# Moving routing and scatter units between the stages of a Mamba/HGRN/PEER block, and giving the gate product of the last loop to GpSimd

## Chip, cores and metric

The kernel runs on one core of a Trainium2 chip, in float32. Its engines are TensorE (PE in the rows; PEld is its weight load), VectorE (DVE), ScalarE (ACT), GpSimd (POOL) and SyncE (SP, which only issues DMAs). The metric is the device time of one execution in microseconds (us).

## The reference, cut to what matters

One block over 1024 tokens of width 1024: RMS norm, an input projection, two mixers side by side (a Mamba-2 SSD with 16 heads in 4 groups, an HGRN2 with 8 heads), an output projection with residual, then a PEER layer and a last RMS norm. The PEER layer is what the change is about:

```python
q = (xt @ w_query).reshape(t, PEER_HEADS, 2, PEER_HALF)
s = jnp.einsum('thpd,hpnd->thpn', q, sub_keys)
s_top, i_top = lax.top_k(s, 16)
cand = (s_top[:, :, 0, :, None] + s_top[:, :, 1, None, :]).reshape(t, PEER_HEADS, 256)
c_top, c_idx = lax.top_k(cand, 16)
expert = idx1 * 128 + idx2            # 16 of 16384 experts a token and head
gate = jax.nn.softmax(c_top, axis=-1)
hid = gelu(einsum('td,thkd->thk', xb, u_table[expert])) * gate
out = einsum('thk,thkd->td', hid, v_table[expert])
```

## The kernel before, in words

Tokens are 8 blocks of 128, in two halves of 4. A program of blocks, each ending when all engines have ended it, runs: norm; for each half SSD (`ssd`), HGRN (`hgrn`), output projection (`mix_out`); then the loop (`peer`). This text calls them SSD 0, HGRN 0, mix 0, SSD 1, HGRN 1, mix 1 and the loop.

**Routing.** Query and keys of one head for two token blocks are a *step* (32 steps): TensorE multiplies the queries and the scores, ScalarE copies them out. A step holds two *units* (64 units, one head of one block). VectorE picks the top 16 of a unit in three parts, `route_keys`, `route_pairs`, `route_place`, with ScalarE's `gates_act` and VectorE's `route_gates` for the softmax.

**Scatters.** The first 32 units (blocks 0 to 3, `DENSE`) are not gathered. GpSimd adds their gates into a zeroed matrix `sel` in HBM (token by expert), with 16 indirect DMAs a unit (`scatter`, L1403). This is its own stream of instructions, one after the other: 96 in mix 0, 48 at the head of SSD 1, 5 behind each of SSD 1's 16 `awide` products, 176 in HGRN 1, 112 in mix 1; 512 in all. All must be in before the loop.

**The loop.** 256 slots, in 16 groups of 16. In slots 0 to 7 of a group TensorE multiplies one tile of 128 experts' u columns with the 512 tokens of the dense half (`peer_ps_d`, L2039), ScalarE applies gelu (L2082), and the result is multiplied by the gates read back from `sel` (`peer_mt`): this is the gate product, L2176, on VectorE, from `dense`. In slots 8 to 15 it multiplies these eight tiles with the v columns into `peer_ps_o` (L2052), which VectorE adds up (L2183). Beside it, each slot handles two gathered rows of the other 32 units (`GATHER`): GpSimd fetches u and v rows of the experts into rings of 5 (`u_row` L1969, `v_row` L1977), VectorE makes a dot product (L2189) and, a slot later, a weighted sum (`combine`, L2200). Each set of 8 slots is m = 0 to 31. Before, the step of m = 0, 2, ... 18 is queried at its slot 0 and scored at its slot 4, and a unit is routed in each m = 1 to 20, its parts in slots 3, 5 and 7, the last behind the slot's combines. VectorE does the product of slot s at the start of slot s+1; TensorE waits for it at the output slot 8 (its k-th matmul there wants the k-th product).

Of the kernel before, what the change touches and what calls it, by code (L numbers as in the profile page):

```python
# [60 lines left out]
BQ = 8  # L61
GATE_LAG = 3
GRP = 4
GE = 8
# [401 lines left out]
def ssd(nc, half, S, w, w_in, w_ssd, par, w_hg, lb_logits, C, hnT, Y, spent, hw, H, state, carry, sel, sel_zeroed, R):  # L466
# [4 lines left out]
    with ExitStack() as ctx:  # L471
# [180 lines left out]
        def _(act):  # L652
# [59 lines left out]
            for n in range(first, end):  # L712
                for c in range(HC):
# [32 lines left out]
                    elif (t - first * HC) % 2 == 1 and (t - first * HC) // 2 < len(ROUTE_CHUNKS):  # L746
                        gates_act(nc, act, R, ROUTE_CHUNKS[(t - first * HC) // 2])

        @block.vector
        def _(dve):  # L750
# [89 lines left out]
            for n in range(first, end):  # L840
# [7 lines left out]
                for c in range(HC):  # L848
# [88 lines left out]
def hgrn(nc, half, G, w_hg, w_out, C, hnT, Y, osq, ysq, first_w, hw, H, state, sel, R):  # L937
# [6 lines left out]
    with ExitStack() as ctx:  # L944
# [132 lines left out]
        def _(act):  # L1077
# [34 lines left out]
            for m in range(first, end):  # L1112
                if m == deep:
                    ken_out(m * HC)
                for c in range(HC):
# [12 lines left out]
                    square_out(t)  # L1128
                    if c == HC - 1 and m < first + HC:
# [9 lines left out]
        def _(dve):  # L1139
            prep = Own(dve, H.own_prep, 1)  # L1140
            for held in atts:
                ins = nc.vector.memset(held[:], 0.0)
# [45 lines left out]
            for m in range(first, end):  # L1188
# [6 lines left out]
                for c in range(HC):  # L1195
# [47 lines left out]
class Route:  # L1243
# [151 lines left out]

def scatter(nc, pool, R, sel, n, ks):
# [36 lines left out]
def mix_out(nc, half, M, x, w_out, mix_w, ffn_w, w_route, u_cols, sel, sel_zeroed, first_w, hw, C, Y, osq, ysq, hnT, R, ut):  # L1433
# [4 lines left out]
    with ExitStack() as ctx:  # L1438
# [10 lines left out]
        if half == 0:  # L1449
# [9 lines left out]
                "p (j a k) -> p j a k", j=2, a=2) for i in range(SCORES - 1))]  # L1459
        else:  # L1460
# [32 lines left out]
        def _(sp):  # L1493
# [39 lines left out]
            load_queries(step + 3)  # L1533
            load_x(first + 3)
            load_keys(step + 3)
            loads(step + 4)
            key_loads(step + 4)
            loads(step + 5)
            key_loads(step + 5)
            for i in TAIL:  # L1540
                load_queries(i)
                load_keys(i)

        @block.tensor
        def _(pe):
# [57 lines left out]
            for b in range(first, end):  # L1603
# [745 lines left out]
```

## Time and profile before

| | us |
|---|---|
| median of 3 runs | 3754.54 (3753.33 to 3755.51) |
| profiled execution, time | 3756.04 |
| profiled execution, span | 3754.3 |
| PE busy | 3378.3 (90%) |
| DVE busy | 2653.5 (71%) |
| POOL busy | 2061.6 (55%) |
| ACT busy | 913.5 (24%) |

The time is 1.7 us above the span of the trace. Busy shares are averages over stages with different limits, so the table alone doesn't say which engine ends a stage. TensorE's granted clock over the whole span is 0.949 of full speed.

### The profile page before, as it was taken

The page shows a single profiled execution, that of the slowest core. Times are in us where ns is not written, and L with a number is a line of the kernel's source. Part 1 is how long each engine was busy: PE and PEld are TensorE (multiplying, and loading weights), DVE is VectorE, ACT ScalarE, POOL GpSimd, SP SyncE. Part 2 cuts the span into 40 slices and gives each one's busy share as a digit, 9 for nine tenths or more (in the row PEclk, how much of TensorE's full clock was granted, in tenths as well). Part 3 has the DMA queues.
Part 4 walks back from the last instruction along what each step waited for, and adds up shares of the span by engine and source line. Part 5 has one row for each costly group of instructions (what it writes and reads, how often), then busy time and mean ns, then how long its engine had stood idle before and what let it go on. Part 6 is the DMA issues. An engine that isn't in the chain of part 4 may idle for free.

```text
span 3754.3 us, 36373 instructions
## 1 busy us (share of the span) xinstructions
PE 3378.3 (90%) x10816; PEld 1900.1 (51%) x10816; DVE 2653.5 (71%) x6220; ACT 913.5 (24%) x2301; POOL 2061.6 (55%) x1618
## 2 busy tenths in 40 slices
PE   7999997992999998197599999999999999999998
PEld 4666774581566777154244444444444444444443
DVE  2476663598698666027488787878787888777888
ACT  3334452220234444022112111111111111111112
POOL 1000000187867788788665555556555656666765
PEclk9999998996999998598799999999999999999999
DMA  3453112253422343342799999999999999999998
GB/s 119 157 219 140 51 57 110 61 117 47 68 46 34 57 63 40 54 97 33 251 378 388 350 348 353 387 355 352 352 385 347 339 375 401 388 402 396 401 404 333
DMA packets 370772, 868.60 MB, mean 231 GB/s; under 512 B 97552, under 2 KB 192016, under 8 KB 363408
## 3 DMA queue, kind: packets, MB, share of 16 engines
q0 software_dynamic: 221184, 537.23, 42.7%
q1 hardware_dynamic: 127840, 246.60, 18.2%
q10 hardware_dynamic: 21552, 82.45, 5.6%
q8 instruction: 87, 1.43, 0.2%
q14 instruction: 109, 0.89, 0.1%
HBM read 828.14 MB, written 38.01 MB: 231 GB/s over the span
## 4 chain that ended last, share of the span: by engine, by line
PE 39%; DMA 5%; DVE 4%; issue 2%; POOL 1%; ACT 0%; DVEq 0%; ACTq 0%; POOLq 0%
PE peer_ps_o L2052 22%; PE peer_ps_d L2039 15%; DMA peer_vr<-in_v_rows,index_g 5%; PE peer_ps_q L2002 2%; DVE Y L2200 1%; DVE peer_ur L2189 1%; POOL peer_ur L1969 0%; DVE lists L1362 0%; DVE route_chosen L1364 0%; DVE lists L1360 0%; POOL peer_vr L1977 0%; DVE Y L2176 0%; DMA wk<-in_w_route 0%; DVE route_ix L1326 0%; DVE route_ix L1318 0%
## 5 line engine op out<-in xcount | busy, mean ns | idle before, releaser
L1403 POOL DMA_INDIRECT sel<-lists x512 | 836.8, 1634 | 292.9 <-issue 151.9
L1969 POOL DMA_INDIRECT peer_ur<-in_u_rows,index_g x512 | 564.1, 1102 | 523.6 <-DVE peer_ur L2189 396.4
L2200 DVE SCALAR_TENSOR_TENSOR Y<-peer_vr,osq,Y 128x1024 f32<-128x1024 f32 x512 | 657.8, 1285 | 143.0 <-DMA peer_vr<-in_v_rows,index_g 142.8
L1977 POOL DMA_INDIRECT peer_vr<-in_v_rows,index_g x512 | 599.2, 1170 | 235.1 <-issue 146.0
L2189 DVE SCALAR_TENSOR_TENSOR peer_ur<-peer_ur,Y 128x1024 f32<-128x1024 f32 x512 | 629.2, 1229 | 43.4 <-DMA peer_ur<-in_u_rows,index_g 43.2
L2052 PE MATMUL peer_ps_o<-hw,Y 128*128 128x512 f32 x1024 | 466.2, 615 | 55.1 <-DVE Y L2176 55.1
L2052 PE MATMUL peer_ps_o<-hnT,Y 128*128 128x512 f32 x1024 | 442.7, 592 | 0.0
L2052 PEld LDWEIGHTS peer_ps_o<-hw,Y 128*128 128x128 f32 x1024 | 201.1, 198 | 315.6 <-issue 249.5
L2052 PEld LDWEIGHTS peer_ps_o<-hnT,Y 128*128 128x128 f32 x1024 | 194.4, 190 | 243.9 <-issue 243.5
L2039 PE MATMUL peer_ps_d<-hnT,held 128*128 128x512 f32 x688 | 302.3, 592 | 0.0
L2039 PE MATMUL peer_ps_d<-hnT,state 128*128 128x512 f32 x688 | 302.3, 592 | 0.0
L2039 PE MATMUL peer_ps_d<-hnT,peer_ut 128*128 128x512 f32 x672 | 295.2, 592 | 0.0
L580 PE MATMUL ssd_ps_piece<-hnT,w_group 128*128 128x512 f32 x512 | 233.2, 610 | 67.9 <-DMA w_group<-in_w_ssd 56.3
L2082 ACT ACTIVATE Y<-peer_ps_d 128x512 f32<-128x512 f32 x128 | 76.4, 597 | 802.4 <-PE peer_ps_d L2039 802.4
L2089 ACT ACTIVATE osq<-osq 128x2 f32<-128x2 f32 x256 | 51.1, 200 | 757.7 <-DVE peer_ur L2189 757.5
L2039 PEld LDWEIGHTS peer_ps_d<-hnT,state 128*128 128x128 f32 x688 | 130.5, 190 | 161.4 <-issue 161.2
L2039 PEld LDWEIGHTS peer_ps_d<-hnT,held 128*128 128x128 f32 x688 | 130.4, 190 | 161.4 <-issue 161.2
L2039 PEld LDWEIGHTS peer_ps_d<-hnT,peer_ut 128*128 128x128 f32 x672 | 127.5, 190 | 158.0 <-issue 157.8
L2176 DVE TENSOR_TENSOR Y<-Y,peer_mt 128x512 f32<-128x512 f32 x128 | 88.5, 691 | 153.4 <-ACT Y L2082 152.5
L580 PEld LDWEIGHTS ssd_ps_piece<-hnT,w_group 128*128 128x128 f32 x512 | 99.9, 196 | 189.6 <-issue 132.2
L559 POOL TENSOR_TENSOR ssd_awide<-ssd_a,tri 128x512 f32<-128x512 f32 x32 | 38.4, 1202 | 284.9 <-PE ssd_ps_rows L630 238.9
L1024 PE MATMUL hg_ps_piece<-hnT,hw 128*128 128x512 f32 x384 | 172.4, 602 | 0.3 <-DMA hw<-in_w_hg 0.3
(335 smaller groups left out, 4775.7 us busy)
## 6 DMA issues: line engine op xcount, KB each, us to landing
sel<-Y ACTq DMA_DIRECT2D x16, 2048.0 KB, 7.1
peer_mt<-sel ACTq DMA_DIRECT2D x64, 512.0 KB, 8.5
hw<-in_v_cols SPq DMA_DIRECT2D x16, 2048.0 KB, 10.9
hnT<-in_v_cols SPq DMA_DIRECT2D x16, 2048.0 KB, 13.9
state<-in_u_cols SPq DMA_DIRECT2D x43, 512.0 KB, 7.7
held<-in_u_cols SPq DMA_DIRECT2D x43, 512.0 KB, 7.7
peer_ut<-in_u_cols SPq DMA_DIRECT2D x42, 512.0 KB, 8.0
w_group<-in_w_ssd SPq DMA_DIRECT2D x32, 512.0 KB, 4.1
```

Of the source, the lines that this page charges most:

```text
L580: mm = nc.tensor.matmul(bank, w[:, k, i * P:(i + 1) * P], hnT[:, half, k, :], start=(k == 0), stop=(k == KT - 1))
L1024: mm = nc.tensor.matmul(bank, w[:, kt, p * P:(p + 1) * P], hnT[:, half, kt, :], start=(kt == 0), stop=(kt == KT - 1))
L1403: nc.gpsimd.indirect_dma_start(sel.rearrange("a i q two (t o) -> (a i q two t) o", o=1), bass.IndirectOffsetOnAxis(ap=R.index_d[:, at, k:k ...
L1969: nc.gpsimd.indirect_dma_start(ur[:, r % RING, :], None, u_rows, bass.IndirectOffsetOnAxis(ap=R.index_g[:, r // TOPK % RQ, r % TOPK:r % TO ...
L1977: nc.gpsimd.indirect_dma_start(vr[:, r % RING, :], None, v_rows, bass.IndirectOffsetOnAxis(ap=R.index_g[:, r // TOPK % RQ, r % TOPK:r % TO ...
L2002: mm = nc.tensor.matmul(ps_q[:, p, :], wq[:, k, p * P:(p + 1) * P], xg[:, k, :], start=(k == 0), stop=(k == KT - 1))
L2039: mm = nc.tensor.matmul(ps_d[:, e % 2, 0:DT], ut[e % UT][:, k, :], xT[:, k, 0:DT], start=(k == 0), stop=(k == KT - 1))
L2052: mm = nc.tensor.matmul(ps_o[:, o % OB, :], ht(e, tb), v_tile(e, side), start=(j == 0), stop=(j == GE - 1))
L2082: nc.scalar.activation(ht(e), ps_d[:, e % 2, 0:DT], ACT.Gelu).then_inc(gelu_done, 1)
L2176: nc.vector.tensor_tensor(h, h, m_tile(e), ALU.mult).then_inc(h_made, 1)
L2189: nc.vector.scalar_tensor_tensor(out=ur[:, s, :], in0=ur[:, s, :], scalar=1.0, in1=Y[:, b, D:MIX], op0=ALU.mult, op1=ALU.mult, accum_out=d ...
L2200: nc.vector.scalar_tensor_tensor(out=hb, in0=vr[:, s, :], scalar=hid[:, c:c + 1], in1=hb, op0=ALU.mult, op1=ALU.add).then_inc(comb_done, 1)
```

## The change

Constants move routing and scatters between the stages, and the code around them follows:

| units of | mix 0 | head of SSD 1 | chunks of SSD 1 | HGRN 1 | mix 1 | loop |
|---|---|---|---|---|---|---|
| routing before | 22 | 4 + 2 | 4 | 0 | 12 | 20 |
| routing after | 14 | 5 + 2 | 5 and a third | 5 and two thirds | 6 | 26 |
| scatters before | 6 | 3 | 5 | 11 | 7 | 0 |
| scatters after | 5 | 3 | 7 | 10 | 7 | 0 |

The steps multiplied in mix 1 fall from 6 to 3, those of the loop rise from 10 to 13. In mix 0 all 16 steps stay; scores of its last 8 now go to places of their own (`later`), so ScalarE needn't wait until VectorE has picked from them. In SSD 1 and HGRN 1 a chunk takes one third of a unit (`part_dve`) where it took half a unit in the first 8 chunks of SSD 1. In the loop the gate product goes from VectorE's `dense` to GpSimd's `gate_product`; a step is queried in odd m, so at slot 8 of a group, and scored at slot 12, and the loads of query weights move with it.

```diff
-BQ = 8
+BQ = 12
-ROUTED_STEPS = HALF_STEPS + 6
-ROUTED_IN = [range(0, 22), range(UNITS // 2, 2 * ROUTED_STEPS)]
-ROUTE_BEFORE, ROUTE_AFTER, ROUTE_CHUNKS = range(22, 26), range(26, 28), range(28, 32)
-SCATTER_MIX0, SCATTER_PROLOGUE, SCATTER_SSD = DENSE[0:6], DENSE[6:9], DENSE[9:14]
-SCATTER_CHUNK = 5
-SCATTER_HG, SCATTER_MIX1 = DENSE[14:25], DENSE[25:]
+ROUTED_STEPS = HALF_STEPS + 3
+ROUTED_IN = [range(0, 14), range(UNITS // 2, 2 * ROUTED_STEPS)]
+ROUTE_BEFORE, ROUTE_AFTER, ROUTE_CHUNKS = range(14, 19), range(19, 21), range(21, UNITS // 2)
+SCATTER_MIX0, SCATTER_PROLOGUE, SCATTER_SSD = DENSE[0:5], DENSE[5:8], DENSE[8:15]
+SCATTER_CHUNK = 7
+SCATTER_HG, SCATTER_MIX1 = DENSE[15:25], DENSE[25:]
...
+def part_dve(nc, dve, R, q):
+    if q // 3 < len(ROUTE_CHUNKS):
+        n = ROUTE_CHUNKS[q // 3]
+        if q % 3 == 0:
+            route_keys(nc, dve, R, n)
+        elif q % 3 == 1:
+            route_pairs(nc, dve, R, n)
+        else:
+            route_place(nc, dve, R, n)
+            route_gates(nc, dve, R, n)
...
-        TURN_AT = 3
+        TURN_AT = 2 * (3 * PH - ROUTED_STEPS)
...
             i = first_step + m // 2
-            return i if m % 2 == 0 and i < STEPS else None
+            return i if m % 2 == 1 and i < STEPS else None
...
-            n = 2 * first_step - 1 + m
-            return n if m >= 1 and n < UNITS else None
+            n = 2 * first_step - 2 + m
+            return n if m >= 2 and n < UNITS else None
...
+            def gate_product(e):
+                pool.wait_ge(gelu_done, e + 1)
+                if e % 2 == 0:
+                    pool.wait_ge(m_in[e // 2 % 2], 16 * (e // 4 + 1))
+                h = ht(e).rearrange("p (q t) -> p q t", t=SELB)
+                nc.gpsimd.tensor_tensor(h, h, m_tile(e), ALU.mult).then_inc(h_made, 1)
...
-            for p in range(PAIRS):
+            for p in range(PAIRS + 1):
+                if p > 0 and (p - 1) % SLOTS < GE:
+                    gate_product((p - 1) // SLOTS * GE + (p - 1) % SLOTS)
                 for r in (2 * p + RING, 2 * p + 1 + RING):
...
             def dense(q):
                 g, s = q // SLOTS, q % SLOTS
-                if s < GE:
-                    e = g * GE + s
-                    dve.wait_ge(gelu_done, e + 1)
-                    if e % 2 == 0:
-                        dve.wait_ge(m_in[e // 2 % 2], 16 * (e // 4 + 1))
-                    h = ht(e).rearrange("p (q t) -> p q t", t=SELB)
-                    nc.vector.tensor_tensor(h, h, m_tile(e), ALU.mult).then_inc(h_made, 1)
-                else:
+                if s >= GE:
```

TensorE at the start of the loop, before (a row is a run of like instructions; `held`, `state` and `peer_ut` are the three places of u columns, `hw` and `hnT` hold the v columns, `peer_ps_q` is the query, `peer_ps_s` the score):

```order
L2002 MATMUL peer_ps_q<-xg,wk 128x256 x16
L2039 MATMUL peer_ps_d<-hnT,state 128x512 x8
L2039 MATMUL peer_ps_d<-hnT,held 128x512 x8
L2039 MATMUL peer_ps_d<-hnT,peer_ut 128x512 x8
L2039 MATMUL peer_ps_d<-hnT,state 128x512 x8
L2012 MATMUL peer_ps_s<-wk,reset 128x128 x4
L2039 MATMUL peer_ps_d<-hnT,held 128x512 x8
L2039 MATMUL peer_ps_d<-hnT,peer_ut 128x512 x8
L2039 MATMUL peer_ps_d<-hnT,state 128x512 x8
L2039 MATMUL peer_ps_d<-hnT,held 128x512 x8
L2052 MATMUL peer_ps_o<-hw,Y 128x512 x32
L2052 MATMUL peer_ps_o<-hnT,Y 128x512 x32
```

The same engine at the same place, after the change (the last eight rows of the group):

```order
L2049 MATMUL peer_ps_d<-hnT,held 128x512 x8
L2049 MATMUL peer_ps_d<-hnT,peer_ut 128x512 x8
L2049 MATMUL peer_ps_d<-hnT,state 128x512 x8
L2049 MATMUL peer_ps_d<-hnT,held 128x512 x8
L2012 MATMUL peer_ps_q<-xg,wk 128x256 x16
L2062 MATMUL peer_ps_o<-hw,Y 128x512 x32
L2022 MATMUL peer_ps_s<-wk,reset 128x128 x4
L2062 MATMUL peer_ps_o<-hnT,Y 128x512 x32
```

The query has moved from ahead of the first u tile to between the last u tile and the first output, and the score to the middle of the outputs.

GpSimd in the loop, before, in any slot:

```order
L1969 DMA peer_ur<-in_u_rows,index_g 128x1024 x2
L1977 DMA peer_vr<-in_v_rows,index_g 128x1024 x2
L1969 DMA peer_ur<-in_u_rows,index_g 128x1024 x2
L1977 DMA peer_vr<-in_v_rows,index_g 128x1024 x2
L1969 DMA peer_ur<-in_u_rows,index_g 128x1024 x2
```

GpSimd in the loop after the change, the last two of a group's eight products and the first slot without one:

```order
L1988 TENSOR_TENSOR Y<-Y,peer_mt 128x512
L1970 DMA peer_ur<-in_u_rows,index_g 128x1024 x2
L1978 DMA peer_vr<-in_v_rows,index_g 128x1024 x2
L1988 TENSOR_TENSOR Y<-Y,peer_mt 128x512
L1970 DMA peer_ur<-in_u_rows,index_g 128x1024 x2
L1978 DMA peer_vr<-in_v_rows,index_g 128x1024 x2
L1970 DMA peer_ur<-in_u_rows,index_g 128x1024 x2
```

The product of a slot stands ahead of the four gathers issued in the next one, and behind those of its own.

## Rows read from the trace of the kernel before

**Rows 1.** Busy time by stretch, HGRN 1 (columns named in the first line).
```profile
core 0: us, PE busy (x) PEld busy (x) DVE busy (x) ACT busy (x) POOL busy (x), PEclk, DMA share, GB/s
1240.00:1510.00 270.00, 253.41 (x1294) 195.57 (x1292) 176.21 (x560) 125.06 (x264) 228.53 (x137) 0.95 0.36 51
1510.00:1585.00 75.00, 2.13 (x10) 1.57 (x9) 1.28 (x4) 0.37 (x2) 57.25 (x38) 0.51 0.23 6
```

**Rows 2.** GpSimd in order of time: start us, us, engine, line, what [idle before].
```profile
733.71 1.82 POOL L1403 DMA_INDIRECT sel<-lists  x1 [122.06 <-DVE lists L1393]
...
918.66 1.55 POOL L1403 DMA_INDIRECT sel<-lists  x1 [0.30 <-issue]
927.13 1.55 POOL L1403 DMA_INDIRECT sel<-lists  x1 [6.92 <-POOLq L1438]
...
1211.63 1.03 POOL L559 TENSOR_TENSOR ssd_awide<-ssd_a,tri 128x512 f32<-128x512 f32 x1 [2.81 <-PE ssd_ps_rows L630]
...
1234.80 1.55 POOL L1403 DMA_INDIRECT sel<-lists  x1 [11.13 <-POOLq L471]
...
1576.99 1.55 POOL L1403 DMA_INDIRECT sel<-lists  x1 [0.30 <-issue]
...
1596.44 1.57 POOL L1403 DMA_INDIRECT sel<-lists  x1 [0.16 <-issue]
...
1810.20 1.55 POOL L1403 DMA_INDIRECT sel<-lists  x1 [0.30 <-issue]
```

**Rows 3.** VectorE in order of time: first instruction of one unit and of the next.
```profile
739.06 0.48 DVE L1315 MAX8 route_ti<-Y 128x8 f32<-128x128 f32 x2
...
748.77 0.48 DVE L1315 MAX8 route_ti<-Y 128x8 f32<-128x128 f32 x2
```

**Rows 4.** VectorE in order of time, head of SSD 1.
```profile
974.73 0.53 DVE L783 COPY hw<-carry 128x12 f32<-128x12 f32 x1 [10.14 <-ACT ssd_rawz L666]
```

**Rows 5.** Busy time by stretch, loop: columns as in rows 1.
```profile
1818.00:1833.40 15.40, 9.62 (x33) 8.11 (x34) 2.47 (x4) 1.28 (x1) 10.81 (x11) 0.65 0.95 382
1833.40:3192.84 1359.44, 1304.37 (x3201) 607.05 (x3201) 1104.63 (x1945) 237.78 (x740) 789.42 (x700) 0.98 0.96 366
3192.84:3742.50 549.66, 549.60 (x1281) 242.76 (x1279) 439.40 (x576) 91.14 (x303) 363.09 (x314) 1.00 1.00 392
```

**Rows 6.** Busy time by stretch: a group with a query, a group without.
```profile
2825.30:2953.84 128.54, 120.57 (x298) 56.51 (x297) 102.39 (x185) 22.12 (x68) 72.36 (x65) 0.96 0.94 353
3247.78:3357.64 109.86, 109.86 (x257) 48.63 (x257) 86.67 (x113) 14.94 (x56) 73.00 (x65) 1.00 1.02 404
```

**Rows 7.** Chain that ended last: start us, us, what.
```profile
2953.84 6.91 PE peer_ps_q L2002 x32
```

**Rows 8.** TensorE in order of time, in the same group.
```profile
2859.51 1.05 PE L2012 MATMUL peer_ps_s<-wk,reset 128*128 128x128 f32 x8
...
2902.01 24.36 PE L2052 MATMUL peer_ps_o<-hw,Y 128*128 128x512 f32 x50 [7.97 <-DVE Y L2176]
```

**Rows 9.** VectorE in order of time, in the same group.
```profile
2839.74 0.69 DVE L2176 TENSOR_TENSOR Y<-Y,peer_mt 128x512 f32<-128x512 f32 x1 [6.86 <-ACT Y L2082]
...
2883.68 1.28 DVE L2200 SCALAR_TENSOR_TENSOR Y<-peer_vr,osq,Y 128x1024 f32<-128x1024 f32 x1 [4.03 <-DMA peer_vr<-in_v_rows,index_g]
...
2890.84 1.22 DVE L2189 SCALAR_TENSOR_TENSOR peer_ur<-peer_ur,Y 128x1024 f32<-128x1024 f32 x1 [2.93 <-DMA peer_ur<-in_u_rows,index_g]
...
2896.39 1.28 DVE L2200 SCALAR_TENSOR_TENSOR Y<-peer_vr,osq,Y 128x1024 f32<-128x1024 f32 x1 [4.32 <-DMA peer_vr<-in_v_rows,index_g]
```

**Rows 10.** Costliest groups: busy us, mean ns | idle before, releaser.
```profile
L2176 DVE TENSOR_TENSOR Y<-Y,peer_mt 128x512 f32<-128x512 f32 x128 | 88.5, 691 | 153.4 <-ACT Y L2082 152.5
```

**Rows 11.** GpSimd, then VectorE, in order of time, in SSD 1.
```profile
1109.20 1.22 POOL L559 TENSOR_TENSOR ssd_awide<-ssd_a,tri 128x512 f32<-128x512 f32 x1 [3.31 <-PE ssd_ps_rows L630]
...
1109.44 1.90 DVE L1360 TENSOR_TENSOR Y<-route_count_u,route_place 128x864 f32<-128x864 uint32 x1
...
1139.01 1.05 DVE L1360 TENSOR_TENSOR Y<-route_count_u,route_place 128x864 f32<-128x864 uint32 x1
```

More of the change, by code:

```diff
@@ L1128, in _ @@
                     square_out(t)
+                    if half == 1:
+                        part_act(nc, act, R, GROUPS * HC + t - first * HC)
                     if c == HC - 1 and m < first + HC:
@@ L1140, in _ @@
             prep = Own(dve, H.own_prep, 1)
+            R.own.eng = dve
             for held in atts:
@@ L1203, in _ @@
                         attend(t + 1)
+                    if half == 1:
+                        part_dve(nc, dve, R, GROUPS * HC + t - first * HC)
                     advance(t)
@@ L1285, in scores @@
     def scores(self, i):
-        return self.slots[i % SCORES] if i < HALF_STEPS else self.sc[:]
+        if i >= HALF_STEPS:
+            return self.sc[:]
+        return self.slots[i % SCORES] if i < PH else self.later[i - PH]
 def hit_of(ap):
@@ L1305, in scores_free @@
 def scores_free(i):
-    return 2 * (i - SCORES + 1) if i < HALF_STEPS else 2 * i
+    if i >= HALF_STEPS:
+        return 2 * i
+    return 2 * (i - SCORES + 1) if i < PH else 0
 def route_keys(nc, dve, R, n):
@@ L1459, in mix_out @@
                 "p (j a k) -> p j a k", j=2, a=2) for i in range(SCORES - 1))]
+            R.later = [Y[:, i // 2, D + i % 2 * HALF:D + (i % 2 + 1) * HALF].rearrange("p (j a k) -> p j a k", j=2, a=2)
+                       for i in range(PH)]
         else:
@@ L1481, in mix_out @@
         step = half * HALF_STEPS
-        EARLY_STEPS = range(step, step + 6)
         TAIL = range(step + 6, HALF_STEPS) if half == 0 else range(0)
+        MORE = half == 0
         w_in = [first_w, *M.w_in]
@@ L1532, in _ @@
             load_keys(step + 2)
-            load_queries(step + 3)
+            if MORE:
+                load_queries(step + 3)
             load_x(first + 3)
[L1535 to L1542, printed above, removed]
+            if MORE:
+                load_keys(step + 3)
+                for i in range(step + 4, HALF_STEPS):
+                    load_queries(i)
+                    load_keys(i)
         @block.tensor
@@ L1651, in _ @@
                 score(i - 1)
-            score(step + 5 + len(TAIL))
+            if MORE:
+                score(HALF_STEPS - 1)
         @block.scalar
@@ L1728, in _ @@
                     x_copy(b - 1, 1)
-                if at == HC - 1:
+                if at == HC - 1 and MORE:
                     query_out(step + 3)
                     gates(unit + 4)
-                    if half == 0:
-                        x_copy(b - 1, 1)
+                    x_copy(b - 1, 1)
                 if at + 1 < HC:
@@ L1754, in _ @@
                 score_out(i - 1)
-                if i > TAIL[0]:
-                    gates(done)
-                    done += 1
-            score_out(step + 5 + len(TAIL))
-            for n in range(done, unit + len(ROUTED_IN[half])):
+            if MORE:
+                score_out(HALF_STEPS - 1)
+            for n in range(unit + 6, unit + len(ROUTED_IN[half])):
                 gates(n)
@@ L1817, in _ @@
                     scale_y(b + 2)
-                if at == HC - 1:
-                    route(unit + 6)
                 dve.wait_ge(M.h_squared, past(b + 1))
@@ L1822, in _ @@
                                         ALU.add).then_inc(M.h_meaned, 1)
-                if at == HC - 1:
-                    route(unit + 7)
                 dve.wait_ge(M.h_rooted, past(b + 1))
@@ L1833, in _ @@
             routed = unit + len(ROUTED_IN[half])
-            for n in range(unit + 8, routed):
+            for n in range(unit + 6, routed):
                 route(n)
-            for n in range(routed - GATE_LAG, routed):
+            for n in range(max(unit, min(routed - GATE_LAG, unit + 6)), routed):
                 route_gates(nc, dve, R, n)
```

46 lines of the change are left out of this document (16 added, 30 removed).

## Prediction

> **What bounds the kernel now.** I read the busy time by stretch first, then for each stretch the engine that ends it, then the chain that ended last in the loop.
>
> In HGRN 1 the arithmetic is over at 1510, and until 1585 only GpSimd works, 57 of 75 us [rows 1]: the block waits for scatters. In order of time GpSimd issues them almost without a break from 733.7 on: mix 0's 96 until 918.7, then a change of block with 6.9 us idle, 176 in HGRN 1 from 1234.8 to 1577.0, 112 in mix 1 from 1596.4 to 1810.2 [rows 2]. The reader is to see pitches of (918.66 - 733.71) / 95 = 1.95 us in mix 0, 342.2 / 175 = 1.955 in HGRN 1 and 213.8 / 111 = 1.93 in mix 1. Mix 0, HGRN 1 and mix 1 end with their scatters; SSD 1 is set by its chunks, 8 of them from 1109.20 [rows 11] to 1211.63 [rows 2], 12.8 us each.
>
> The loop runs from 1818.0 to 3742.5, 1924.5 us [rows 5]. From 3192.8 TensorE never pauses: 549.6 us of work in 549.66 us, and a group without a query takes 109.86 us [rows 5, 6]. Before that, groups with routing lose time. A query is 6.91 us [rows 7], a score about 0.9 (1.05 with its modelled end [rows 8]), so a group with both should take 117.7 us; the one shown takes 128.5, with 8.0 us of TensorE idle [rows 6]. The idle time ends on VectorE's gate product (7.97 us), and the 50 matmuls behind it take 24.4 us [rows 8], where 50 at the later pace (109.86 / 256 = 0.429) take 21.5; the group's granted clock is 0.96 against 1.00 [rows 6]. Over the stretch up to 3192.84: 11 groups of 109.86, 9 queries, 10 scores and some 2 us of transposes make 1281.7 us of 1359.4; 77.7 us are lost, 55.1 idle and 22.6 at a slower clock [rows 5].
>
> Why the product is late: in the group shown VectorE waits 4.03, 2.93 and 4.32 us for gathered rows, then routes a third of a unit, then comes to the eighth product [rows 9]. Earlier in the group it had waited 6.86 us itself, for gelu, as the query stood ahead of the first tile [rows 9]. VectorE is busy 102.4 of those 128.5 us [rows 6]. The two wait for each other in turn.
>
> **Change, part by part.**
>
> *Mix 0.* One unit fewer to scatter: 16 x 1.95 = 31.2 us off the end, if nothing else ends later. VectorE had 8 units more than now, at 748.77 - 739.06 = 9.71 us each [rows 3], so its tail falls by 78 us and stays behind GpSimd's. TensorE keeps its 16 steps; its score copies lose a wait. -31.
>
> *Head of SSD 1.* A fifth unit ahead of the group's preparation, 9.7 us. VectorE idles 10.1 us there for ScalarE's copies [rows 4]: this hides it. 0, and up to +10 if ScalarE came early.
>
> *Chunks of SSD 1.* GpSimd's chunk becomes 1.2 us of `awide` with its gap and 7 scatters at 1.91 us: 14.6 us. Its first block instruction to the sixteenth `awide` is 927.1 to 1211.6, 284.5 us [rows 2]. With 48 scatters at 1.90 (91 us) and 15 chunks of 14.6 (219) it is 310, +25.5 us. VectorE takes 3.2 us of routing a chunk in place of 4.9 in the first eight, 3.2 in place of 0 in the rest; GpSimd's 14.6 us covers it, except perhaps in the last chunk. +26.
>
> *HGRN 1.* 160 scatters for 176: -16 x 1.955 = -31.3. The routing added, 5 and two thirds units or 55 us, lies in 17 of 32 chunks. VectorE is busy 176 of 270 us and TensorE 253 [rows 1]; the arithmetic is over 67 us before the last scatter, and would still be over some 10 us before it if all of the 55 came on top. Sum up to mix 1: -31 + 26 - 31 = -36; 1 us back for the last chunk. **-35**.
>
> *Mix 1.* VectorE loses 6 units (58 us), TensorE three steps; both lie beside the 112 scatters, which stay. At best the pitch falls from 1.93 to the 1.85 of undisturbed ones (1.55 + 0.30 [rows 2]), -9; I take **-2**.
>
> *Loop, TensorE's work.* Three queries and scores more: 3 x 7.8 = +23.4. The start needs no query weights: now 15.4 us pass before the first tile, 9.6 of them a slow first query [rows 5]; the wait of 5.8 goes, the slow clock falls on the first tile (2.7 over a warm query). Work after: 16 x 109.86 + 13 x 7.8 + 2.7 + 2 + 1 = 1865 us.
>
> *Loop, what becomes of the 77.7 us.* The query now lies between the eighth tile and the first output, and in that output seven eighths can run before the eighth product is wanted: 12.9 us of cover, where it was 6. In the group shown the combines of slot 7 end at 2897.6, 9.7 us after the eighth tile. GpSimd then has one or two gathers and the product: about 2.5 us, 12.2 in all. VectorE's place-part no longer stands ahead. It just fits, without any gain in the waits for rows; moving the 1 MB of query weights away from slot 6 should make these shorter.
>
> *Loop, VectorE.* It gives up 8 products a group at 0.69 us [rows 10] (0.6 apart in sequence), -4.8. But GpSimd's product makes VectorE wait: beside `awide` (same size, 1.22 us) a VectorE product took 1.90 us, where its like takes 1.05 [rows 11], so 0.85 us a product, +6.8. A group with routing is 102.4 - 4.8 + 6.8 = 104 us of 117.7; 13 us are left for the 11.3 of waits for rows. The Trainium skill, SBUF — State Buffer, Who interferes with whom, says that a VectorE instruction with two SBUF inputs and a GpSimd one that reads SBUF exclude each other, the second fully blocked. By that rule the price is the whole 1.22 us, 9.8 a group: 107 of 117.7, and the sum stays; this trace shows 0.85. The same skill, GPSIMD Engine Reference, Engine selection, advises against two-input products on GpSimd, about twice as slow; the trace has 1.03 to 1.22 us against 0.69.
>
> *Loop, GpSimd.* Busy 72.4 us and 65 gaps of 0.3 make 92 of 128.5 [rows 6, 2]; 8 products with gaps at 1.2 to 1.4 add 11: 103 of 117.7, or of 109.9 in late groups. It has room, but little. Bound of the product from above: 1.22 plus a wait of 1.28 for VectorE's instruction, 8 x 2.5 = 20, 112 us, still below 117.7 and over 109.9.
>
> *Transfers.* The late group moves 404 GB/s with a DMA share of 1.0 over 109.86 us, 44.4 MB [rows 6]. With 1.1 MB of query in 117.7 us it is 387 GB/s, so it fits too.
>
> I leave 1.5 us a routing group (13 x 1.5 = 20) for what is left of stalls and slow clock: 1865 + 20 = 1885, **-40** (0 a group gives -60, 4.5 a group -1). Sum: -35 - 2 - 40 = -77. The profiled execution, 3756.0 with its 1.7 us outside the span, would be 3679; it lies 1.5 above the median of the runs, which goes from 3754.5 to **3677**.
>
> **Rivals.**
> 1. *The stall stays, as it is made by transfers.* For it: three near-full engines and a DMA share near 1, and 13 groups that route instead of 10. Against it: the cover doubles. With 3 to 6 us a group the loop is 1904 to 1943, -20 to +19: 3697 to 3736.
> 2. *Slower: GpSimd becomes the loop's bound.* Its queue is in order: a product waits for gelu, four gathers wait behind it, VectorE for their rows, the next product for VectorE. It decides if a routing group takes 7.5 us over 117.7 (13 x 7.5 = 97, eating 37 + 60), which is a pitch of 125.2, as now. At 128.5 the time is 3754.5 - 37 + 81 = 3799. For it: 103 to 112 us of work in order. Against it: gathers now wait for VectorE's dot at the same place anyway.
> 3. *Front part falls short.* HGRN 1's arithmetic is stretched past its scatters, or the chunks take 16 us: 10 to 20 lost, 3687 to 3697.
> 4. *More than forecast:* no stall left, scatters at 1.85 us: 3754.5 - 42 - 9 - 62 = 3642.
> 5. *It does nothing of what it says:* gains cover only the added queries. That is rival 1 at its end.
>
> **How the numbers follow.** Forecast with rival 3 (3655 to 3697) 0.65; rival 4, below 3655, 0.08; rival 1 0.17; rival 2 0.10, most of it above 3762. The range 3640 to 3720 leaves out rival 2, half of rival 1 and little else. Some 0.2%, 7.5 us, is what a measurement here can tell. Faster by more: 0.65 + 0.08 + 0.16 = 0.89; within: 0.03; slower: 0.08.
>
> **What would show it.** Mix 0's last scatter near 888; `awide` 14.6 apart in SSD 1; HGRN 1's last scatter near 1541, with 10 to 40 us of GpSimd alone before it; mix 1 as long as before, VectorE idle at its end; the loop's routing groups at 118 to 120 us with a clock of 1.00, VectorE's instructions near the products 0.6 to 0.9 longer. I am wrong if TensorE still waits at slot 8, if a product on GpSimd takes over 2.5 us, or if groups without routing exceed 110 us.

## The result: 3713.4 us, faster by 1.0%, and the profile after

| | before | after |
|---|---|---|
| median of runs, us | 3753.93 (3747.84 to 3755.51, 4 runs) | 3713.43 (3711.16 to 3720.9, 4 runs) |
| ratio, 95% interval | | 0.9899 [0.9881, 0.9916] |
| profiled execution: time, span | 3756.04, 3754.3 | 3720.9, 3719.2 |
| start of the loop (after: of its first tile), us | 1818.0 | 1786.13 |
| loop to the last matmul | 1924.5 | 1921.2 |

The change gains 40.5 us where 77 were forecast, and 3677 lies below all of its runs. The profiled execution is the slowest of the four, 7.5 us over their median; I come back to that.

**Front.** GpSimd in order of time, after: the first scatter of SSD 1, the sixteenth `awide`, the first and last scatter of HGRN 1, the last of mix 1, the first gather. They answer to [rows 2].

```profile
893.82 1.55 POOL L1420 DMA_INDIRECT sel<-lists  x1 [5.77 <-POOLq L1455]
...
1202.85 1.61 POOL L559 TENSOR_TENSOR ssd_awide<-ssd_a,tri 128x512 f32<-128x512 f32 x1
...
1228.66 1.57 POOL L1420 DMA_INDIRECT sel<-lists  x1 [10.25 <-POOLq L471]
...
1547.56 1.55 POOL L1420 DMA_INDIRECT sel<-lists  x1 [0.31 <-issue]
...
1778.18 1.55 POOL L1420 DMA_INDIRECT sel<-lists  x1 [0.30 <-issue]
1786.85 1.01 POOL L1970 DMA_INDIRECT peer_ur<-in_u_rows,index_g  x1 [7.12 <-POOLq L1455]
```

SSD 1 begins at 893.8 where it was 927.1, so mix 0 gave 33 us (forecast 31). The sixteenth `awide` is 309 us behind it (forecast 310, was 284.5), and no idle time stands before it any more: GpSimd sets the chunks. HGRN 1's last scatter is at 1547.6, where 1541 was forecast; its pitch is (1547.56 - 1228.66) / 159 = 2.006 us, not 1.955, 8 us over 159 scatters. That is a matter of this execution: in e1, the same instructions up to the loop, it is 1.96 us (1228.8 to 1540.5).

Busy time by stretch, HGRN 1 after, against [rows 1]:

```profile
core 0: us, PE busy (x) PEld busy (x) DVE busy (x) ACT busy (x) POOL busy (x), PEclk, DMA share, GB/s
1500.00:1530.00 30.00, 9.19 (x69) 8.49 (x69) 10.47 (x42) 3.68 (x13) 25.12 (x17) 0.67 0.22 1
1530.00:1550.00 20.00, 0.00 (x0) 0.00 (x0) 0.00 (x0) 0.00 (x0) 16.07 (x11) 0.50 0.23 0
```

From 1530 on GpSimd works alone: the routing put into HGRN 1 stayed beside the scatters, which still end the block.

**Loop.** Busy time by stretch after, in order: the first group, a usual one, that with the transposes, the last three. Against [rows 6]:

```profile
1786.00:1919.70 133.70, 124.16 (x297) 57.70 (x298) 83.11 (x101) 17.41 (x59) 92.85 (x79) 0.93 0.99 388
1919.70:2037.36 117.66, 117.66 (x297) 55.61 (x297) 101.73 (x171) 22.34 (x68) 84.67 (x72) 1.00 0.99 380
...
2391.07:2516.46 125.39, 120.08 (x313) 56.94 (x313) 104.51 (x177) 23.94 (x72) 89.38 (x76) 1.00 0.97 369
...
3344.91:3468.11 123.20, 114.34 (x257) 49.77 (x257) 103.17 (x177) 21.56 (x66) 88.23 (x74) 0.94 0.95 361
3468.11:3589.15 121.04, 111.67 (x257) 49.07 (x257) 92.35 (x115) 19.99 (x64) 90.14 (x73) 0.96 0.96 373
3589.15:3707.30 118.15, 112.82 (x257) 49.26 (x255) 92.23 (x113) 26.46 (x71) 83.04 (x66) 0.97 0.89 323
```

Seven of the routing groups came down to the 117.7 us that their work takes, as forecast, with TensorE never idle and the granted clock at 1.00 in the one shown; four more take 118.4 to 119.9. What is new is mostly at the ends: the first group takes 133.4 us, and groups without a query, which had taken 109.9 us [rows 6], now take 118 to 123. TensorE in order of time in the first of them, against [rows 8]:

```profile
3399.68 5.31 PE L2062 MATMUL peer_ps_o<-hw,Y 128*128 128x512 f32 x12
3408.84 2.07 PE L2062 MATMUL peer_ps_o<-hw,Y 128*128 128x512 f32 x2 [3.85 <-POOL Y L1988]
3415.92 24.72 PE L2062 MATMUL peer_ps_o<-hw,Y 128*128 128x512 f32 x50 [5.01 <-POOL Y L1988]
```

TensorE waits for the seventh product, and again for the eighth, now for GpSimd: 8.9 us. The other 4.5 us over 109.9 go with the granted clock, 0.94 in that group where it was 1.00. Costliest groups after, columns as in [rows 10]:

```profile
L2203 DVE SCALAR_TENSOR_TENSOR Y<-peer_vr,osq,Y 128x1024 f32<-128x1024 f32 x512 | 690.6, 1349 | 178.3 <-DMA peer_vr<-in_v_rows,index_g 124.5 <-issue 53.4
L2192 DVE SCALAR_TENSOR_TENSOR peer_ur<-peer_ur,Y 128x1024 f32<-128x1024 f32 x512 | 675.3, 1319 | 109.1 <-DMA peer_ur<-in_u_rows,index_g 107.8 <-DVE route_place L1355 0.2
```

In the kernel with the product back on VectorE (e1, below) the same two take 1282 and 1229 ns. The difference is 512 x (67 + 90) ns = 80 us, 0.63 us for each of the 128 products.

Here is what each group of the loop takes, from the start of its first u tile to that of the next one, in us, for all kernels of this study (an edit of each is told below):

| kernel | 0 | 1 to 12, those over 118.0 | 13 | 14 | 15 | loop |
|---|---|---|---|---|---|---|
| before | 117.8 | 123.6 to 128.5 in 1 to 8; 117.2, 114.9, then 109.9 | 109.9 | 110.1 | 110.0 | 1909.2 |
| after | 133.4 | 125.4 (5), 118.4 to 119.9 in four | 123.2 | 121.0 | 118.3 | 1921.2 |
| e1, product on VectorE | 126.5 | 125.4 (5) | 118.8 | 109.9 | 110.0 | 1884.9 |
| e2, that in 13 to 15 | 132.8 | 123.8 (4), 125.4 (5), 118.2 (11) | 117.9 | 109.9 | 110.0 | 1898.1 |
| e3, before + product on GpSimd | 120.4 | 116.7 to 129.1 | 118.7 | 116.9 | 118.2 | 1949.8 |
| e4, before + query in odd m | 127.4 | 125.4 (2); 113.0 (10), 109.9 (11, 12) | 109.9 | 110.0 | 110.0 | 1856.7 |
| e5, e1 + transposes in m = 9 | 126.4 | 119.4 (4) | 118.4 | 109.9 | 110.0 | 1878.5 |
| e6, two fills for the product | 129.4 | 125.4 (5) | 122.0 | 116.4 | 110.0 | 1897.6 |
| e7, half of the products on GpSimd | 125.8 | 125.4 (5), 119.1 (6) | 120.3 | 113.9 | 110.0 | 1891.8 |
| e8, front moves alone | 117.7 | 122.8 to 127.2 in 1 to 11, 115.9 (12) | 116.5 | 109.9 | 110.0 | 1942.0 |
| e9, e5 + parts in slots 1, 3, 5 | 126.4 | 119.4 (4) | 109.9 | 114.8 | 110.0 | 1874.9 |
| e10, after + transposes in m = 9 | 133.9 | 120.2 (5), 118.2 to 119.9 in seven | 120.6 | 122.6 | 117.2 | 1915.6 |

(Before, e3 and e8 begin with a query ahead of the first tile, 6.9 us and more, which the last column leaves out for them: 1909.2 is 1924.5 less 15.3, and those are the wait for the query weights and the query itself.)

### The profile page after: what moved, and what is told of

Its sections match the earlier page's. It is cut to its first block, busy times and chain, and to the rows that moved or that the text cites. A ratio compares the mean times of both kernels' runs of the same rounds, so it can differ in the third digit from the quotient of the medians.

```text
span 3719.2 us, 36340 instructions
## 1 busy us (share of the span) xinstructions
PE 3382.6 (91%) x10816; PEld 1901.5 (51%) x10816; DVE 2690.8 (72%) x6092; ACT 928.7 (25%) x2312; POOL 2312.7 (62%) x1746
## 4 chain that ended last, share of the span: by engine, by line
PE 41%; issue 3%; DMA 3%; POOL 3%; DVE 2%; ACT 0%; POOLq 0%; ACTq 0%; DVEq 0%
PE peer_ps_o L2062 23%; PE peer_ps_d L2049 16%; DMA peer_vr<-in_v_rows,index_g 3%; PE peer_ps_q L2012 1%; POOL peer_ur L1970 1%; DVE Y L2203 1%; POOL Y L1988 1%; POOL peer_vr L1978 1%; PE peer_ps_s L2022 0%; DVE peer_ur L2192 0%; DVE Y L2220 0%; PE peer_ps_t L2031 0%; ACT xg L2086 0%; DVE wk L2220 0%; ACT osq L2103 0%
## 5 line engine op out<-in xcount | busy, mean ns | idle before, releaser
L1970 POOL DMA_INDIRECT peer_ur<-in_u_rows,index_g x512 | 636.9, 1244 | 334.6 <-DVE peer_ur L2192 218.8
L2203 DVE SCALAR_TENSOR_TENSOR Y<-peer_vr,osq,Y 128x1024 f32<-128x1024 f32 x512 | 690.6, 1349 | 178.3 <-DMA peer_vr<-in_v_rows,index_g 124.5
L2192 DVE SCALAR_TENSOR_TENSOR peer_ur<-peer_ur,Y 128x1024 f32<-128x1024 f32 x512 | 675.3, 1319 | 109.1 <-DMA peer_ur<-in_u_rows,index_g 107.8
L2062 PE MATMUL peer_ps_o<-hw,Y 128*128 128x512 f32 x1024 | 455.5, 604 | 37.2 <-POOL Y L1988 37.2
L580 PE MATMUL ssd_ps_piece<-hnT,w_group 128*128 128x512 f32 x512 | 232.6, 608 | 48.5 <-DMA w_group<-in_w_ssd 36.4
```

Of the source, the lines that this page charges most:

```text
L580: mm = nc.tensor.matmul(bank, w[:, k, i * P:(i + 1) * P], hnT[:, half, k, :], start=(k == 0), stop=(k == KT - 1))
L1970: nc.gpsimd.indirect_dma_start(ur[:, r % RING, :], None, u_rows, bass.IndirectOffsetOnAxis(ap=R.index_g[:, r // TOPK % RQ, r % TOPK:r % TO ...
L2062: mm = nc.tensor.matmul(ps_o[:, o % OB, :], ht(e, tb), v_tile(e, side), start=(j == 0), stop=(j == GE - 1))
L2192: nc.vector.scalar_tensor_tensor(out=ur[:, s, :], in0=ur[:, s, :], scalar=1.0, in1=Y[:, b, D:MIX], op0=ALU.mult, op1=ALU.mult, accum_out=d ...
L2203: nc.vector.scalar_tensor_tensor(out=hb, in0=vr[:, s, :], scalar=hid[:, c:c + 1], in1=hb, op0=ALU.mult, op1=ALU.add).then_inc(comb_done, 1)
```

## The experiments

Theory T1, formed from the trace after: wherever no query lies between the last u tile and the first output, GpSimd's eighth product comes late, because four gathers and a product a slot take GpSimd more than TensorE's 6.87 us; and beside each product VectorE loses time. Rivals: R1, handing the product over is what gained, and the late groups are its price; R2, transfers set the pace.

**e1: the product back on VectorE, all else changed.**

```diff
-                if p > 0 and (p - 1) % SLOTS < GE:
+                if False:
                     gate_product((p - 1) // SLOTS * GE + (p - 1) % SLOTS)
...
-                if s >= GE:
+                if s < GE and True:
+                    e = g * GE + s
+                    dve.wait_ge(gelu_done, e + 1)
...
+                    nc.vector.tensor_tensor(h, h, m_tile(e), ALU.mult).then_inc(h_made, 1)
```

> The changed kernel with one part undone: the gate product is back on VectorE in all groups, at the start of the next slot; queries stay in odd m and all moves between stages stay. Theory T1 (GpSimd's queue, with four gathers and a product a slot at a pitch of about 8.0 us against TensorE's 6.87, delivers the eighth product late wherever no query lies in between, and makes VectorE's instructions longer): the last three groups return from 118 to 123 us to 109.9, -33, the first group gives some 5 back, the routing groups keep their 12.9 us of cover and lose at most 1 us each as VectorE is slower by 4.8 us of products but quicker by 5 us of blocked port: 3670 to 3690, so faster than the changed kernel's 3713. Rival R1 (the routing groups need the product off VectorE, and it was the handover that gained): they go back to some 125 us, 12 x 7 = +84, less 33: 3755 to 3765. Rival R2 (transfers set the loop): 3710 to 3715.

Measured: 3671.29 us (3666.95 to 3678.7), ratio 0.9789 [0.9768, 0.9811]. R1 and R2 fall: with the product where it was, groups 1 to 12 take 117.7 us but for that with the transposes, and the last two 109.9 and 110.0. T1's time came true, though group 13 stayed at 118.8 us where it had 109.9. Handing the product to GpSimd costs 3713 - 3671 = 42 us by the medians. The medians of the kernel before that were timed beside the two differ by 4.9 us of this (3753.9 and 3749.0), which leaves 37, and the loops of the two profiled executions differ by 36.3.

**e2: the product on VectorE in groups 13 to 15 alone.** The two conditions read `(p - 1) // SLOTS < 13` and `g >= 13`.

> The changed kernel, with the gate product on VectorE in groups 13 to 15 alone (the three without a query), on GpSimd in groups 0 to 12. T1: these three take 109.9 us each again in place of 123.2, 121.0 and 118.2, so -33: 3680, TensorE's granted clock there 1.00 and no wait at slot 8. R2 (the late groups are slow as their rows and tiles come late): 3710 to 3715, with waits for DMA in these groups.

Measured: 3685.53 us (3677.12 to 3687.75), ratio 0.9822 [0.9801, 0.9843], 5.5 us over T1's 3680. The last two groups are at 109.9 and 110.0, group 13 at 117.9. The three gave 24.7 us, not 33: 8 us of group 13's delay are not GpSimd's (TensorE waits 5.8 us there for VectorE's eighth product; see e9). In groups 1 to 12 GpSimd's products cost little: e2 is 6.1 us longer than e1 in group 4 and 1.4 us in the other eleven together; 6.3 more are in group 0.

**e3: the kernel before with the product on GpSimd alone.** The inverse of e1's edit, on the kernel before.

> The kernel before, with one part of the change: the gate product on GpSimd; queries stay in even m and nothing moves between stages. T1: the six groups without a query, which took 109.9 us, take 118 to 123, +50 to +75, and the routing groups, whose query stands ahead of the first tile and covers nothing, gain nothing: 3800 to 3830, slower. R1 (handing the product to GpSimd is what gained): routing groups 118 in place of 125, 10 x 7 = -70, late groups up by 60: 3740 to 3750. If the product on GpSimd costs nothing by itself: 3690.

Measured: 3801.18 us (3787.22 to 3804.86), ratio 1.0132 [1.0109, 1.0154]: slower, as T1 has it. Groups 11 to 15 take 117 to 119 us in place of 109.9 to 110.1, and groups 0 to 9 together gain 4 us.

**e4: the kernel before with the query in odd m alone.**

```diff
-        TURN_AT = 3
+        TURN_AT = 4
...
-            return i if m % 2 == 0 and i < STEPS else None
+            return i if m % 2 == 1 and i < STEPS else None
...
-            n = 2 * first_step - 1 + m
-            return n if m >= 1 and n < UNITS else None
+            n = 2 * first_step - 2 + m
+            return n if m >= 2 and n < UNITS else None
```

> The kernel before, with one part of the change: queries in odd m, so between the last u tile and the first output, with the units and the transposes following; the product stays on VectorE and nothing moves between stages. T1: the cover for the eighth product grows from 6 to 12.9 us, the stalls of some 8 us in ten groups mostly go, and the clock with them: -50 to -75: 3680 to 3705. R1 (only the handover helps): 3750 to 3757.

Measured: 3689.09 us (3681.72 to 3690.7), ratio 0.9837 [0.9818, 0.9856]. These few lines give 60 us, one and a half times what the whole change gives.

**e5: e1 with the transposes in m = 9.** `TURN_AT = 9`.

> As the kernel with all products on VectorE (median 3671), and the four groups of transposes moved from m = 10 (slots 2 to 5, where TensorE computes u tiles and ScalarE has a gelu in each slot) to m = 9 (slots 10 to 13, as before the change). Theory T2 (the transposes wait for ScalarE's copies, which stand behind gelu there; 125.4 us for that group against 117.7): the group returns to some 118.5 us, -7: 3664. Rival (transposes cost some 8 us anywhere in the group with a query at slot 8): 3671.

Measured: 3663.42 us (3660.73 to 3671.18), ratio 0.9787 [0.9771, 0.9803]. The group that now holds them, 4, takes 119.4 us, and group 5 is back at 117.7: 1.7 us for what took 7.7. TensorE in order of time in the changed kernel's group 5 shows what is saved: ScalarE copies each set out only behind its gelu, and TensorE waits to overwrite it.

```profile
2413.88 0.66 PE L2031 MATMUL peer_ps_t<-ident,Y 128*128 128x128 f32 x4 [1.77 <-ACT xg L2086]
2414.37 7.03 PE L2049 MATMUL peer_ps_d<-hnT,held 128*128 128x512 f32 x16
2423.17 0.66 PE L2031 MATMUL peer_ps_t<-ident,Y 128*128 128x128 f32 x4 [1.77 <-ACT xg L2086]
```

**e6: fills in place of the product.** The gate product is left out, so the outputs are of a constant.

```diff
                 h = ht(e).rearrange("p (q t) -> p q t", t=SELB)
-                nc.gpsimd.tensor_tensor(h, h, m_tile(e), ALU.mult).then_inc(h_made, 1)
+                nc.gpsimd.memset(m_tile(e), 0.5)
+                nc.gpsimd.memset(h, 0.5).then_inc(h_made, 1)
```

> The changed kernel with the gate product left out altogether: in its place in GpSimd's queue, behind the same waits and with the same release, stand two fills with a constant, of the gates' tile and of the activations' tile, which read no SBUF (a fill of this size takes 0.52 us in the trace of before, so some 1.1 us for both against the product's 1.35). The output tiles are then computed from a constant. It splits T1 in two. T1a (time in GpSimd's queue alone makes the eighth product late): late groups stay at 116 to 121 us, 3700 to 3710. T1b (what costs is that product and VectorE's two-input instructions shut each other out, so that VectorE and the gathers that wait for it are late): VectorE's dots and sums return to 1.22 and 1.28 us at most 1.33, the late groups to 110, the first to 117: 3665 to 3680.

Measured: 3684.87 us (3677.6 to 3688.91), ratio 0.9835 [0.982, 0.985]. This lies between T1a and T1b, 5 us above T1b's range, so neither does alone. Group 15, which routes nothing, shows how they add. GpSimd in order of time there, in e6, three starts of a product's substitute:

```profile
3573.27 0.94 POOL L1978 DMA_INDIRECT peer_vr<-in_v_rows,index_g  x1 [0.30 <-issue]
3574.22 0.54 POOL L1988 MEMSET peer_mt<- 128x512 f32 x1
3574.68 0.54 POOL L1989 MEMSET Y<- 128x512 f32 x1
3575.38 1.51 POOL L1970 DMA_INDIRECT peer_ur<-in_u_rows,index_g  x1 [0.16 <-issue]
...
3581.11 0.54 POOL L1989 MEMSET Y<- 128x512 f32 x1
...
3587.96 0.55 POOL L1989 MEMSET Y<- 128x512 f32 x1
```

and in the changed kernel, VectorE and then GpSimd, in the same group:

```profile
3597.35 2.96 DVE L2203 SCALAR_TENSOR_TENSOR Y<-peer_vr,osq,Y 128x1024 f32<-128x1024 f32 x1 [1.59 <-issue]
...
3606.56 2.28 DVE L2203 SCALAR_TENSOR_TENSOR Y<-peer_vr,osq,Y 128x1024 f32<-128x1024 f32 x1
...
3614.67 2.29 DVE L2192 SCALAR_TENSOR_TENSOR peer_ur<-peer_ur,Y 128x1024 f32<-128x1024 f32 x1
```
```profile
3597.93 1.28 POOL L1988 TENSOR_TENSOR Y<-Y,peer_mt 128x512 f32<-128x512 f32 x1
3599.38 1.77 POOL L1970 DMA_INDIRECT peer_ur<-in_u_rows,index_g  x1 [0.16 <-issue]
3602.22 1.27 POOL L1970 DMA_INDIRECT peer_ur<-in_u_rows,index_g  x1 [1.08 <-DVE peer_ur L2192]
3603.80 0.95 POOL L1978 DMA_INDIRECT peer_vr<-in_v_rows,index_g  x1 [0.30 <-issue]
3605.05 1.27 POOL L1978 DMA_INDIRECT peer_vr<-in_v_rows,index_g  x1 [0.30 <-issue]
3606.34 1.42 POOL L1988 TENSOR_TENSOR Y<-Y,peer_mt 128x512 f32<-128x512 f32 x1
...
3614.45 1.42 POOL L1988 TENSOR_TENSOR Y<-Y,peer_mt 128x512 f32<-128x512 f32 x1
```

The fills keep TensorE's pitch, 6.4 and 6.9 us; the products are 8.4 and 8.1 apart, though one is only 0.3 to 0.4 us longer than both fills (1.0). The VectorE instruction beside a product takes 2.28 to 2.96 us where 1.22 to 1.28 is its own time; two of the three began 0.22 us behind the product, the third 0.58 us ahead of it. The products take at most 1.42. Over the loop, one tile's instructions in the three kernels (count: shortest/median/longest ns), first the changed one, then e1, then e6:

```profile
L2203 DVE SCALAR_TENSOR_TENSOR Y<-peer_vr,osq,Y x512: 1270/1283/2993, 1809.9 to 3709.3; 128x1024 f32<-128x1024 f32 x171
```
```profile
L2210 DVE SCALAR_TENSOR_TENSOR Y<-peer_vr,osq,Y x512: 1272/1279/1323, 1802.4 to 3665.4; 128x1024 f32<-128x1024 f32 x171
```
```profile
L2204 DVE SCALAR_TENSOR_TENSOR Y<-peer_vr,osq,Y x512: 1273/1281/1351, 1801.4 to 3677.3; 128x1024 f32<-128x1024 f32 x171
```

So it is the product, not GpSimd being busy, that stretches VectorE: 2993 ns against 1323 and 1351. The product goes with a second lengthening, on GpSimd itself. Costliest groups, the gathers of u rows, in the changed kernel, e1 and e6 (columns as in [rows 10]):

```profile
L1970 POOL DMA_INDIRECT peer_ur<-in_u_rows,index_g x512 | 636.9, 1244 | 334.6 <-DVE peer_ur L2192 218.8
```
```profile
L1970 POOL DMA_INDIRECT peer_ur<-in_u_rows,index_g x512 | 566.7, 1107 | 519.6 <-DVE peer_ur L2199 401.4
```
```profile
L1970 POOL DMA_INDIRECT peer_ur<-in_u_rows,index_g x512 | 579.9, 1133 | 383.5 <-DVE peer_ur L2193 274.6
```

To issue them takes 70 us more than in e1 and 57 more than in e6; the gather right behind a product takes 1.62 us on the mean, right behind the fills 1.19. From the first to the eighth product of group 15 the changed kernel takes 56.2 us: 28 gathers 38.4, seven products 9.4, gaps 8.4. In e6 it is 48.5: gathers 34.0, fills 7.0, gaps 7.5. So of the 7.7 us between them the gathers carry 4.4, the product's own length 2.4, and gaps and waits 0.9.

Of the 36.3 us by which the changed loop is longer than e1's, e6 keeps 12.7 (1897.6 - 1884.9): queue time, in groups 0, 13 and 14. The other 23.6, two thirds, go away as the product becomes two fills. That is more than the shut-out alone, as the fills are also shorter: it is an upper bound for it.

**e7: half of the products on GpSimd,** those of slots 0 to 3, with a semaphore of their own.

> The changed kernel with the products of slots 0 to 3 of each group on GpSimd and those of slots 4 to 7 on VectorE. After slot 3 GpSimd's queue has its pitch of before, under 6.9 us, and four slots in which to catch up. T1a: nothing is late at slot 8, late groups 109.9: 3675 to 3680, equal to all products on VectorE but for the transposes. T1b: half of the blocked time stays on VectorE, but as it has room in the middle of a group little of it reaches slot 8: 3675 to 3690. If GpSimd's products cost in proportion to their number whatever the slot: (3671 + 3713) / 2 = 3692.

Measured: 3684.74 us (3679.47 to 3688.4), ratio 0.9841 [0.9826, 0.9856]: above T1a's range, in that of T1b, and 7 us from proportion. Group 15 is whole again (110.0), 13 and 14 lose 1.5 and 4.0 us against e1. The loops say more than the medians: e7's is 6.9 us longer than e1's, where proportion asks for 18. So it speaks against T1a alone and, as far as one execution of each can, against proportion. TensorE's waits there name VectorE's product: what was blocked in slots 0 to 3 had not been caught up.

**e8: the front moves alone,** with 13 steps in the loop: e5 with the query back in even m.

> The changed kernel with its moves of routing and scatters between the stages alone: the product on VectorE and the query in even m, ahead of the first u tile, as before, with 13 steps in the loop and the transposes in m = 9. T1 (the front saves 32 us, and each step that it moves into the loop costs 7.8 us of TensorE and, with the query in the old place, the old stall of some 5 us too): -32 + 3 x 12.5 = +5: 3750 to 3760. If the moved units are covered in the loop: 3749 - 32 = 3717. If only the stall does not come: 3740.

Measured: 3746.05 us (3738.42 to 3759.82, 12 runs), ratio 1.0 [0.9986, 1.0014]. 4 us under T1's range, and the same as before. What the front gives, the three steps take: from the first tile on the loop is 1942.0 - 1909.2 = 33 us longer. Without the new place of the query, the moves between the stages are worth nothing.

**e9: the parts of a routed unit in slots 1, 3, 5** of each eight (softmax in slot 4), on e5.

> The kernel with all products on VectorE and the transposes in m = 9 (median 3663), with the three parts of a routed unit in slots 1, 3 and 5 of each eight in place of 3, 5 and 7 (the softmax on ScalarE in slot 4 in place of 5). In the kernel without this edit group 13, which routes two units and has no query, takes 118.4 us in place of 109.9. T3 (the last part, in slot 7, stands ahead of the eighth product on VectorE): group 13 falls to 110 to 112, nothing else moves, -6 to -8: 3656. Rival (it is the sum of VectorE's work up to slot 8 that makes the product late, wherever it stands): 3663.

Measured: 3666.8 us (3661.4 to 3670.58), ratio 0.9766 [0.9747, 0.9785], the same as e5. Group 13 falls from 118.4 to 109.9 as T3 says, but group 14 rises from 109.9 to 114.8, with a wait of 3.3 us for VectorE's product. The loop gains 3.6 us of the 6 to 8 expected, and the median shows nothing. Why group 14 now waits, I have not settled.

**e10: the changed kernel with the transposes in m = 9.**

> The changed kernel (median 3713) with the transposes in m = 9 alone, the product still on GpSimd. T2 (they cost 7.7 us in m = 10 whoever makes the product): -7: 3706. Rival (with GpSimd's products the groups around them have no room, so that the stall only moves): 3713. Against the kernel with all products on VectorE and the transposes in m = 9, 3663, the difference is then the price of the product on GpSimd alone: 42.

Measured: 3706.21 us (3693.96 to 3709.44), ratio 0.9862 [0.984, 0.9885]: T2's number, though the group that the transposes left gives only 5.2 us (125.4 to 120.2) and the one that now holds them takes 1.5 more (118.4 to 119.9); the loop is 5.6 us shorter. Against e5 it isolates the product: 3706 - 3663 = 43 us by the medians, but the kernel before was 10 us slower beside e10 than beside e5 (3755.5 and 3745.7). Against e9, timed beside e10 and as fast as e5, it is 39, and the loops of e10 and e5 differ by 37.1: the price that e1 shows.

## Why the prediction was half right

**Mix 0, head of SSD 1, chunks, HGRN 1: right.** -33 for -31; +25 for +26; HGRN 1 had a pitch 0.05 us longer than reckoned in this execution, 8 us. The loop's first tile came 31.9 us earlier in the profiled execution, not 37. This part varies from one execution to the next: the same instructions up to the loop put its first tile at 1786.1, 1778.6, 1774.4, 1777.7, 1777.5, 1771.3, 1778.3 and 1777.0 in the changed kernel, e1, e2, e6, e7, e5, e9 and e10, against 1811.4 in e4, which has the front of before. That is 25 to 40 us, 33.8 on the mean. The forecast of -37 stands within it, and rival 3 explains some 3 us on the mean.

**Mix 1: right** that its routing lies beside the scatters: they take 210.8 us in place of 213.8, -3 for -2.

**Loop, TensorE's work, and the cover: right.** "It just fits": 12.9 us of cover for the late product, and e4 alone gives 60 us by it. e1 is the forecast's kernel but for the engine of the product, and its loop takes 1884.9 us; 1885 had been forecast, with 20 us for stalls. Over 117.7 and 109.9 it loses 8.8 in group 0, 7.7 at the transposes and 8.9 in group 13, of which 2.7 and 2 were in the work term: 20.7. The other routing groups lose nothing. So the sum of the allowance was right by luck: it had been meant as 1.5 us in each of 13 groups, and three losses of which two had other causes made it up.

**The step that failed is "Loop, GpSimd": "103 of 117.7, or of 109.9 in late groups. It has room, but little."** It set 16 slots of work against 16 slots of time. But the eight products lie in eight slots in a row, with no query to stretch them, and TensorE wants the last at their end. From the first product to the eighth TensorE takes 7 x 6.87 = 48.1 us, GpSimd 55.4 in group 13 (its products start at 3359.18 to 3414.60) and 56.2 in group 15. The eight slots without products, where it has room, come too late. In groups with a query the 6.9 us hide just this, which is why most look as forecast. The sum itself was too small as well: in groups 13 and 14 GpSimd is busy 88.2 and 90.1 us, with the gaps about 109 to 111. The product's 1.2 to 1.4 us were right; what had been put at nothing is that gathers beside products take longer to issue. The upper bound given there, 112 us "over 109.9", was the sign; I did not let it into the sum.

**The port term was of the right kind and mis-placed.** I had charged VectorE +0.85 us a product, against its 0.6 saved; 0.63 was measured on the mean, and nothing was saved. The average hides that a VectorE instruction which meets a product is delayed by 1.0 to 1.7 us in the rows of group 15. The 1.7 is more than the product's own 1.28, so one product does not explain all of it. The Trainium skill, SBUF — State Buffer, section Who interferes with whom, says that such a pair excludes each other and the second is fully blocked. On the exclusion e6 against the changed kernel agrees, with 2993 against 1351 ns at the longest, where the one early row [rows 11] had shown 0.85; on which of the two is held up it does not always: the instruction that took 2.96 us had begun before its product. I had priced that rule in VectorE's busy time of a group, where there is room. It costs in GpSimd's queue, ahead of the eighth product. One link is that VectorE is late with a dot and GpSimd's next gather waits for it (1.08 us in the rows of group 15), but it is the small one: over that group's eight products gaps and waits give 0.9 us against e6, the longer gathers 4.4, and over the loop the u gathers wait less for VectorE's dots than in e1 (218.8 us for 401.4). Why a gather takes longer to issue beside a product is open; no run here isolates it.

**Two smaller misses.** The late groups were taken at 109.86, the time of a group without routing; group 13 routes two units without a query, and even with the product on VectorE it takes 118 to 119 us, by the place of the third part (e9). And the transposes were "some 2 us", which was true of output slots and is 7.7 among u tiles (e5).

**Rivals.** Rival 2 had the mechanism (a product waits for gelu, gathers wait behind it, VectorE for their rows) but was tied to routing groups; it came true at the ends of the loop instead, at some 40 us where it needed 97 to decide. Rival 1's time, 3697 to 3736, holds the result with another cause: its stall is gone in the groups it spoke of. Two of the three tests fired: "groups without routing exceed 110 us", and "TensorE still waits at slot 8", in groups 0 and 13 to 15; a product took at most 1.68 us.

In sum, by medians: the query's new place -60 (e4), the front and its three steps -18 with it (e1 against e4) and nothing without it (e8), the product on GpSimd +42 (e1): -36, against the -40.5 measured. The rest is the 4.9 us between the two medians of the kernel before; with each kernel set against the one timed beside it, the product's price is 37. The best kernel here leaves that last part out and keeps the transposes in output slots: e5, 3663 us.

## What to carry to other kernels

Check an in-order queue against the shortest stretch in which its results are wanted, not against the loop's period: here 103 of 109.9 us looked like enough on the average, and 7.9 to 8.0 us a slot against 6.87 was too much where it counted. When a change has several parts, price each alone: one moved instruction gave 60 us, and the part meant to relieve VectorE cost some 40. Work for which an engine waits is best put where a stretch of other work follows that does not need it.

## What the runs showed of the hardware

- A GpSimd product of 128x512 with two SBUF inputs (1.27 to 1.68 us) and a VectorE instruction with two SBUF inputs get in each other's way: the latter took up to 2993 ns in place of 1283 (changed kernel), mostly but not only where it began second. With fills by GpSimd in the same place the same instruction (L2203, L2204 in e6) stays at 1351 or less.
- GpSimd's issue of a gather of u rows has no fixed length, with or without products, but is longer with them: 939/948/2002 ns (shortest/median/longest) in e1, 939/980/2002 in e6, 939/1239/2003 in the changed kernel; means 1107, 1133 and 1244. What lengthens it was not tested.
- Identical instructions up to the loop took 1771 to 1786 us in eight profiled executions, 0.8%, with scatters at a pitch of 1.85 us when nothing else ran and up to 2.01 beside arithmetic.
